# A transformer block with 32 experts on one core: the last down weights are loaded at the start, slots are added in place, down biases are added on the way out of PSUM

## The reference

```python
logits = (hf @ w_router).astype(f32) + b_router.astype(f32)
top_logits, top_idx = lax.top_k(logits, TOP_K)          # 4 of 32
top_w = jax.nn.softmax(top_logits, axis=-1)
...
def expert_block(args):
    xb, e = args
    gu = xb @ w_gate_up[e] + b_gate_up[e]
    gate = jnp.minimum(gu[:, ::2], SWIGLU_LIMIT)
    up = jnp.clip(gu[:, 1::2], -SWIGLU_LIMIT, SWIGLU_LIMIT)
    act = (up + 1.0) * (gate * jax.nn.sigmoid(gate * SWIGLU_ALPHA))
    return act @ w_down[e] + b_down[e]
...
y = jax.ops.segment_sum(ys.astype(f32) * slot_w[:, None], slot_tok, num_segments=n_tok)
```

## Time and profile before

| | us |
|---|---|
| median of 3 runs (1922.38 to 1924.10) | 1923.28 |
| the profiled execution, its time | 1925.91 |
| the profiled execution, its span | 1923.9 |

### The profile page before, as it was taken

The page is one execution under the profiler, slowest core; times in us unless marked ns, Lnnn a source line. Parts: engine busy times, 40 slices in busy tenths (PEclk is TensorE's granted clock), DMA queues, the critical chain, the costliest instruction groups (busy, mean ns, idle before and its releaser), DMA issues.

```text
span 1923.9 us, 40758 instructions
## 1 busy us (share of the span) xinstructions
PE 1877.7 (98%) x17206; PEld 948.9 (49%) x17206; DVE 634.5 (33%) x1168; ACT 333.3 (17%) x596; POOL 262.0 (14%) x305
## 2 busy tenths in 40 slices
PE   7999999999999999999999999999999999999995
PEld 3455555555555444445454545445454545444453
DVE  2463554635623100034231313222231313222226
ACT  3223323323323000021010101101011101101002
POOL 0010010000100000013212122121212122121200
PEclk9999999999999999998999999999999999999998
DMA  9211111111101412337999999999999999999995
GB/s 374 89 66 31 43 45 50 45 51 44 45 10 39 177 66 88 116 131 275 370 420 418 420 417 419 418 420 419 417 420 418 420 418 420 418 419 419 418 400 210
DMA packets 82217, 495.45 MB, mean 258 GB/s; under 512 B 15188, under 2 KB 15868, under 8 KB 28256
## 3 DMA queue, kind: packets, MB, share of 16 engines
q1 hardware_dynamic: 72656, 478.49, 61.6%
q0 software_dynamic: 9488, 15.94, 2.2%
HBM read 478.00 MB, written 24.53 MB: 261 GB/s over the span
## 4 chain that ended last, share of the span: by engine, by line
PE 92%; DVE 3%; DMA 1%; DVEq 1%; SPq 1%; ACT 1%; issue 1%; ACTq 0%
PE ps L1081 34%; PE ps L584 21%; PE ps L1096 17%; PE ps L579 10%; PE ps L604 2%; PE ps L803 2%; DMA arena<-expert_rows 1%; DVE arena L1525 1%; DVE arena L1528 1%; PE ps L1017 1%; PE ps L921 1%; PE ps L916 1%; PE ps L896 0%; PE ps L688 0%; PE ps L773 0%
## 5 line engine op out<-in xcount | busy, mean ns | idle before, releaser
L1081 PE MATMUL ps<-arena 128*32 128x512 f32 x5952 | 646.8, 593 | 2.3 <-DVE arena L1525 2.3
L1081 PEld LDWEIGHTS ps<-arena 128*32 128x32 f32 x5952 | 233.4, 110 | 396.5 <-issue 393.0
L584 PE MATMUL ps<-hT,arena 128*128 128x512 f32 x768 | 350.9, 598 | 1.2 <-DVE arena L1528 0.9
L1096 PE MATMUL ps<-arena,hT 128*32 128x256 f32 x6144 | 339.7, 380 | 8.9 <-DMA arena<-in_w_dn 8.9
L1096 PEld LDWEIGHTS ps<-arena,hT 128*32 128x32 f32 x6144 | 240.2, 110 | 115.2 <-issue 27.6
L1525 DVE TENSOR_TENSOR arena<-ps,arena 128x768 f32<-128x768 f32 x64 | 58.3, 953 | 584.2 <-PE ps L1081 584.2
L584 PEld LDWEIGHTS ps<-hT,arena 128*128 128x128 f32 x768 | 139.0, 191 | 144.3 <-issue 140.1
L2252 POOL DMA_INDIRECT expert_rows<-hT,six x90 | 90.4, 1004 | 684.0 <-ACT hT L1163 665.7
L1163 ACT ACTIVATE hT<-arena 128x768 f32<-128x768 f32 x31 | 48.6, 1567 | 434.0 <-DMA arena<-h_rows,gix 434.0
L584 PE MATMUL ps<-arena 128*128 128x512 f32 x256 | 118.5, 603 | 4.4 <-DVE arena L1525 2.2
L2240 POOL DMA_INDIRECT arena<-h_rows,gix x93 | 95.3, 1025 | 49.0 <-POOL gix L2237 27.2
(11 more groups left out here) (250 smaller groups left out, 1293.8 us busy)
## 6 DMA issues: line engine op xcount, KB each, us to landing
arena<-in_w_gu SPq DMA_DIRECT2D x256, 1024.0 KB, 15.4
arena<-in_w_dn SPq DMA_DIRECT2D x128, 1024.0 KB
arena<-in_w_pair SPq DMA_DIRECT2D x16, 1024.0 KB, 4.9
arena<-in_w_merge SPq DMA_DIRECT2D x16, 1024.0 KB, 4.8
expert_rows<-oaT SPq DMA_DIRECT2D x4, 2048.0 KB, 25.1
arena<-expert_rows SPq DMA_DIRECT2D x16, 512.0 KB, 14.4
arena<-in_x SPq DMA_DIRECT2D x8, 512.0 KB, 6.8
arena<-in_w_qb SPq DMA_DIRECT2D x4, 768.0 KB, 4.5
```

The source lines that it names most:

```text
L584: ins = pe.matmul(region(name)[:, cols], lhsT, rhs, start=(k == 0), stop=(k == n - 1))
L1081: ins = pe.matmul(gu[32 * j:32 * (j + 1), g, :], columns[:, g, k, :], ring[k][:, 512 * j:512 * (j + 1)], start=(k == 0), stop=(k == KD - 1))
L1096: ins = pe.matmul(yd[32 * j:32 * (j + 1), g, 0:256], aT[:, g, 2 * c + k, :], ring[8 + c][:, D * k + 256 * j:D * k + 256 * (j + 1)], start= ...
```

## The change

- **Last down weights.** Expert 31's four down chunks get four buffers of their own (`last_down`, in memory that is free after the router). SP loads them while expert 0 runs: two behind the storing of the last normed rows, two behind the collecting products, all ahead of the loads of the slot table. The last down products (`last_expert_down`) write to the banks of the up products and read their columns from a buffer of their own (`last_aT`).
- **Down bias.** `expert_rows` on VectorE replaces ScalarE's `rows_out`: a small copy and a transpose spread the bias of the expert along rows, and one addition takes the products out of PSUM. `tile_bias`, `weight_columns`, `wmT`, `bb4` and the loads of `bdn` go.
- **Slots.** They are added into `x2` in place of `acc`. VectorE adds slots 0 and 1 ahead of the last activations and slots 2 and 3 between the last two `expert_rows`. Rows of extra blocks go to a table of their own (`late_rows`), which is cleared at the start as well.
- **End.** `AWAY` goes: for each tile `add_parts`, `root`, `finish` one after another on VectorE. The masks signal per expert (`joins_done`).
- **Rows.** The normed rows are written in a permuted order (four strided instructions per tile), so that gathered rows can be transposed directly; ScalarE's `permute` goes. `first_tokens` collects expert 0's rows with tokens as output rows; VectorE transposes them out of PSUM. `table_places(3)` comes behind that transpose, `table_places(2)` ahead of `choose(3)`.
- **Mixer.** `token_rows` and GpSimd's sources go. `along_rows` (a VectorE transpose of a vector spread over 32 columns) makes the same rows; the decays' part (`decay_arguments`) runs at the end of the scan before.

```diff
@@ sync
+            last_down_weights(0)
+            ready(sp, f"lg{NT - 1}")
+            last_down_weights(1)
+            ready(sp, "x0_0", "x0_1")
+            sp.wait_ge(h2_st, 16 * NT)
+            last_down_weights(2)
+            last_down_weights(3)
             sp.wait_ge(table_set, 16 * NT * TOPK)
...
-            for k in range(2):
-                early_slot(k)
-            down_weights(NE - 1, NE - 1)
-            for k in range(2, TOPK):
-                early_slot(k)
+            for k in range(TOPK):
                 sp.wait_ge(gu_used, 8 * (NE - 1) + 2 * k + 2)
                 sp.wait_ge(scattered, 16 * QUADS * min(NE - TOPK + 1 + k, JOINED[0]))
@@ tensor
+            def last_expert_down():
+
+                pe.wait_ge(last_down_in, 64)
+                pe.wait_ge(gu_free, NE)
+                pe.wait_ge(aT_done, NE)
+                for c in range(4):
+                    down_products(last_aT, last_down[c], c, into=gu)
@@ vector, mixer
+            def decay_arguments(i):
+
+
+                along_rows(gc_rows, gc_half[:, i])
+                dv.drain()
+                tt(dt_, gc_rows, fac[:, i, F_GC, :].unsqueeze(2).broadcast_to([P, NC, CHUNK]), ALU.subtract)
+                dv.drain()
+                dv.tensor_scalar(dt_, dt_, 0.0, None, ALU.min).then_inc(arg_done, 1)
@@ vector, router
-                stt(h2[:, t, :], x2[:, t, :], r4[:, 1, t:t + 1], nrow).then_inc(h2_done, 1)
+                for j in range(4):
+                    quarter = slice(256 * j, 256 * (j + 1))
+                    natural = lambda a: a[:, quarter].rearrange("p (m b) -> p m b", b=KD)
+                    ins = stt(h2[:, t, quarter].rearrange("p (b m) -> p m b", b=KD), natural(x2[:, t]), r4[:, 1, t:t + 1], natural(nrow))
+                ins.then_inc(h2_done, 1)
@@ vector, experts
+            def expert_rows(n, e, into=ys, products=yd, passed=0):
+
+
+                dv.tensor_copy(down_now, down_columns[:, bass.ds(8 * e, 8)])
+                dv.drain()
+                dv.transpose(down_rows, down_now.unsqueeze(2).broadcast_to([P, 8, 32]))
+                dv.drain()
+                dv.wait_ge(dn_used, 4 * n + 4)
+                if into is ys and not first(n):
+                    dv.wait_ge(scattered, 16 * QUADS * (n - passed))
+                tt(into.rearrange("p (g s) -> p g s", g=QUADS), products[:, :, 0:256],
+                   down_rows.unsqueeze(1).broadcast_to([P, QUADS, 256]), ALU.add).then_inc(ys_done, 1)
@@ vector, end
+            for k in range(2):
+                early_slot(k)
             activations(NE - 1)
-            activation_columns(NE - 1)
-            dv.wait_ge(row_in, 48)
+            dv.transpose(last_aT.rearrange("p g b m -> p (g b m)"), act.rearrange("p g f -> p (g f)")).then_inc(aT_done, 1)
+            dv.wait_ge(row_in, 32)
...
-            dv.drain().then_inc(wm_done, 1)
-            for k in range(TOPK - 1):
-                dv.wait_ge(slot_in[k], 16 * NT)
-                add_slot(k)
-                dv.sem_inc(early_sums, 1)
+                dv.drain().then_inc(joins_done, 1)
+            expert_rows(NE - 2, NE - 2)
+            for k in range(2, TOPK):
+                early_slot(k)
+            expert_rows(NE - 1, NE - 1, into=last_ys, products=gu)
...
             for t in range(NT):
-                dv.wait_ge(rows_in[t], 48)
-                add_rows(TOPK - 1, t)
-                dv.drain()
-                add_parts(acc, t).then_inc(sum_done, 1)
+                add_parts(t).then_inc(sum_done, 1)
                 dv.sem_inc(bo_kept, 1)
-                if t:
-                    root(t - 1)
-            for t in range(AWAY, NT - 1):
+                root(t)
                 finish(t)
```

More of the change, by code:

```diff
@@ L47 @@
 JOINED = (NE - 2, NE - 1)
-AWAY = 2
 SMALL = 128 + ROWS
@@ L249, in build @@
         osb, WT = U, ar3(28.5, 2, SEQ)
-        sg, sa, dt_, cm, qk = (chunks(29.5 + n / 2) for n in range(5))
+        gc_rows, beta_rows, dt_, cm, qk = (chunks(29.5 + n / 2) for n in range(5))
         vnew = ar3(30.5, 2, P)
@@ L1076, in up @@
                     pe.wait_ge(chunk_in[k], 16 * n + 16)
-                    if first(n) and k % 4 == 0:
-                        after(f"x0_{k // 4}")
+                    if first(n) and k == 0:
+                        after("x0_0")
+                        after("x0_1")
                     for g in range(QUADS):
@@ L1085, in up, with down_products, down @@
                         beside[k]()
-            def down(n):
+            def down_products(columns, weights, c, into=yd):
+                for k in range(2):
+                    for g in range(QUADS):
+                        for j in range(4):
+                            ins = pe.matmul(into[32 * j:32 * (j + 1), g, 0:256], columns[:, g, 2 * c + k, :],
+                                            weights[:, D * k + 256 * j:D * k + 256 * (j + 1)],
+                                            start=(c == 0 and k == 0), stop=(c == 3 and k == 1))
+                ins.then_inc(dn_used, 1)
+            def down(n, loads_before=0):
                 if not first(n):
@@ L1452, in _ @@
             ac.activation(e4[:, :, :], e4[:, :, :], ACT.Exp).then_inc(e4_done, 1)
-            for b in range(2):
-                ready(ac, f"x0_{b}")
-                copy(first_xT[:, :, 4 * b:4 * b + 4, :], region(f"x0_{b}")[:, 0:4 * ROWS].rearrange("p (b g m) -> p g b m", b=4, g=QUADS)).then_inc(frees(f"x0_{b}"), 1)
-            def permute(n):
-                ac.wait_ge(gathered, 16 * QUADS * n)
-                if not isinstance(n, int) or n > 1:
-                    ac.wait_ge(xT_done, n - 1)
-                copy(xgp.rearrange("p (g b m) -> p g m b", g=QUADS, b=KD), xg.rearrange("p (g m b) -> p g m b", g=QUADS, b=KD)).then_inc(permuted, 1)
             def gate(n):
@@ L2115, in _ @@
             spread_bias(1)
-            with dv.Fori(1, NE - 1) as n:
+            activations(1)
+            token_columns(2)
+            activation_columns(1)
+            expert_rows(0, 0)
+            spread_bias(2)
+            with dv.Fori(2, NE - 1) as n:
                 activations(n)
@@ L2163, in _ @@
                         activation_columns(j + NE)
+                        expert_rows(j + NE, e, passed=len(JOINED))
                 dv.wait_ge(again_in, 16 * NT * TOPK)
-                for k in range(TOPK - 1):
+                for k in range(TOPK):
                     add_slot(k)
```

274 lines of the change are left out of this document (116 added, 158 removed).

## The result

Eleven runs of each: the changed kernel takes 1927.06 us (1925.42 to 1928.98), the kernel before 1923.64 (1922.16 to 1925.45). The ratio is 1.0019, with a 95% interval of 1.0012 to 1.0027: about 3.4 us slower. Timed again in two more comparisons the ratio was 1.0018 (1.0009 to 1.0027) and 1.0016 (1.0007 to 1.0025).

A forecast was written before the change was run, and what follows sets the result against it. TensorE, gapless through the experts' loop, was taken as the bound, DMA second. Mixer -3.8, router -3.1 and end +6.7 sum to -0.2 us, giving 1923.1 us on the median; range 1913 to 1931.

The forecast's parts named there:

- its own bound of 0.2%: Whole kernel: a difference within 3.8 us can't be told from no change; 1919.4 to 1927.1 us counts as the same.
- the signs: Wrong if TensorE's gap behind expert 30 is under 10 us, up products wait for chunks, or table loads land after 896.
- The bound and the loop: Experts' loop: TensorE gapless at 30.96 us per expert; VectorE's extra 1.5 us per expert hidden; 3.7 us queue slack holds.
- The queue's estimate: DMA entering the loop: 10.0 us moved loads plus 3.1 less 13.2 idle, about 0; queue as long as before within 2.
- The mixer: Head pairs ahead of the router: fewer products and VectorE operations, less eight added copies; 3.8 us gained, bounds 0 and 7.9.
- the hold that it weighed and set aside: Mixer's tiny VectorE operations: a quadrant change holds the next instruction; by that rule the gain is about 1 us smaller.
- Router to second expert: From first expert's row collection to the second expert's start: first expert 5.8 us earlier, second 3.1; bounds 6.4 and -2.
- rival (c): Router and mixer: table late behind moved loads, or small mixer gains absent; 3 to 5 us lost, 1927.5 us; chance 0.15.
- The end: Behind expert 30's down products: TensorE waits for VectorE's slot additions and activations instead of weights; 6.7 us lost.
- The sum: Whole kernel: -3.8 - 3.1 + 6.7 = -0.2 us, 1923.1 us on the median; forecast's chance 0.45.
- (a): Rival at the end: slots land early, the new wait is short and the weight wait goes; 1914.5 us; chance 0.20.
- (b): Rival in the loop: DMA queue never recovers from the moved 10.0 us; 1929 us with 6 us left; chance 0.20.

The follow-up runs named there:

- e7: Changed kernel with the four last down loads made a second time behind expert 1's up weights, TensorE waiting for all eight: 1938.29 us, ratio 1.0036.
- e6: Kernel before with the mixer's edits alone; router, loop and end as before: 1926.84 us beside 1930.32, ratio 0.9982.
- e9: Changed kernel, unedited, timed again with a profile of another execution: 1927.37 us.
- e10: Changed kernel, unedited, timed again with another profile, beside two edited versions on one chip: 1926.91 us.
- e2: Changed kernel with the loads of the last two quarters of the last down weights issued behind the slot table's loads: 1930.1 us, ratio 1.0006.
- e12: Changed kernel with the last down weights' loads put back at the end: 1924.81 us beside the changed kernel's 1926.91, ratio to before 1.0002.
- e1: Changed kernel with VectorE adding slots 0 and 1 behind expert 30's output rows, not ahead of the last activations: 1917.22 us, ratio 0.9943.

## Why the prediction was wrong where it was

The forecast of 1923.1 was 3 to 4 us low: it said a fraction of a microsecond faster, and the kernel got 3.4 us slower. By its own bound of 0.2% the result, 1927.06, sits at the edge between the same and slower; the interval of that comparison leaves no doubt of the sign. None of the signs came by which it would have called itself wrong: the gap is 17.55 us, no up product waits for a chunk, and VectorE uses the table at 892.26, ahead of 896. The mechanism it named, two gains ahead of the loop paid back by VectorE's new wait, is what the traces show. Two terms were off, and a third was right in part by luck.

**The bound and the loop: right.** Periods of 30.96 us on both sides, no wait in the loop, landings of 25.6 where about 25 was forecast. The first expert starts 13.6 us behind the last tile's transposes instead of 19.0, near the 5.8 less that was estimated. The queue's estimate (10.0 + 3.1 - 13.2, about 0) fits, and e7 confirms the limit of 28.4.

**The mixer: right in size, in part by luck.** Forecast 3.8; 3.5 by e6's time, 5.1 by the traces. The thirteen traces with the new mixer end it anywhere from 862.3 to 866.0 and only one has the old, so the 5.1 could be 2 us off. Inside the term two errors stand against each other. The eight small copies take 1.49 us, not 0.95, and the eight tiny products of a pair take 1.32:

```profile
69.17 1.49 DVE L1568 COPY gc_half<-fac 32x32 f32<-32x32 f32 x8
...
240.37 1.32 DVE L1479 TENSOR_TENSOR beta_half<-fac,r 32x8 f32<-32x8 f32 x8
...
242.52 0.17 DVE L1657 TENSOR_SCALAR lf<-r 128x8 f32<-128x8 f32 x1
```

Each of these copies lasts 0.175 us and starts 0.19 after the one before it, so nothing overlaps. The sixteen copies of the kernel before last 0.174 and start 0.115 apart, but the prediction misread them: by the order of their loops they change quadrant three times in all, where the eight change at every step. So the hold that it weighed and set aside is there. Against that, "two GpSimd products go too" was priced at nothing. In the kernel before VectorE's small operations beside them are long:

```profile
245.10 1.05 POOL L2205 TENSOR_TENSOR arena<-mkc,lf 128x512 f32<-128x512 f32 x1
245.16 1.01 DVE L1673 TENSOR_SCALAR lf<-r 128x8 f32<-128x8 f32 x1
```

The same operation takes 0.17 us in the changed kernel, and another beside GpSimd's first product takes 1.05. In the three pairs behind the first some 2 us of VectorE's time go to this in the kernel before, and they go away with GpSimd's products.

**Router to second expert: the term that failed.** Forecast 3.1; the first pair of traces gives 0.8 (45.3 to 44.5), e9 and e10 2.1 and 1.5. Counted from the last tile's transposes, the gathered rows were to be there 37.4 us on (906.1 less 868.73) and are there at 40.5, so 3.1 later than forecast. Two steps failed.

The larger one is the time of the last table write. The prediction's "the last table writes start behind the row transpose and end about 0.8 earlier" means 18.2 (before: 19.0). It goes out at 20.3, 2.1 later than that: GpSimd has stood 6.66 us for VectorE's addresses of the last tile when it starts the four writes at 879.56. VectorE makes them behind the row transpose, and that waits for the collecting products. In all twelve traces with the new order this write goes out 19.3 to 22.1 us behind the transposes, with the weights early or late, so the moved loads have no part in it.

The smaller one is where the moved loads were put: "two of the moved 1 MB loads go ahead of the table's loads on SP's queue" priced the delay of the table's *loads*, at 2.1 us. What they delay are the table's *writes*, GpSimd's, on another queue, through the DMA engines that they keep busy. The loads wait 2.7 us longer for the write and bring the rows after 15.4 instead of 15.0, so 3.1 stand where 2.1 were allowed. Over the seven traces the interval is 4.6 on average, 2.5 over before's: the price was nearly right, its place was wrong. This is rival (c)'s place, with another victim. The steps behind the rows took 3.9 instead of 4.8. Together 2.1 + 1.0 - 0.9, the 2.2 to 2.3 us that the term is short.

The prediction weighed the Trainium skill (DMA: Bandwidth & Descriptors, section "Queues, rings and completion order") here: on a DMA engine several queues take turns. The queues of the changed kernel in 884 to 885:

```profile
q1 hardware_dynamic: 58, 0.43, 102.6%
q0 software_dynamic: 16, 0.00, 1.1%
```

That is 58 weight packets on 16 engines, 0.28 us each; a table write has 32 packets, two an engine. By turns alone a write would be held some 0.6 us, an estimate; the runs show 2 to 3. So taking turns by itself does not account for what a small write waits beside a full queue; what does was not shown.

**The end: 1.6 us short.** Forecast 6.7 lost, the traces give 8.3 (67.15 us from expert 30's down products to the end of the span, against 58.8). 1.1 of it is one step: slot 0 was to be there 1.3 earlier against TensorE's work, since no 0.5 MB load goes ahead of it; its addition starts 11.3 us after expert 30's down products begin, against 11.5 for the full count before. From slot 0 to the end the prediction's steps give 55.3, the trace 55.9. One trace is a draw here as well: in e9 the end loses 7.0 us and slot 0 comes after 10.0, as forecast, in e10 it loses 10.5 and slot 0 comes after 12.1.

**The sum.** -5.1 - 0.8 + 8.3 = 2.4, where -3.8 - 3.1 + 6.7 = -0.2 stood. The times differ by 1 us more than the traces (3.4), since the profiled execution of before took 1925.91, 2.3 over its median, and that of after 1928.08, 1.0 over. Over the three traces of the changed kernel the mixer gives 5.9, the router 1.4, the loop 0.3, and the end loses 8.6: the router is 1.7 short and the end 1.9, and the mixer gives back 2.1. Where the profiled execution of before spent its 2.3 us over the median is open; a forecast that is summed on one trace and put onto the median carries that much doubt in every term.

**The rivals.** (a) is out: slot 0 comes at 1870.4, not near 1859, and the gap is 17.55 us. (b) did not occur, but e7 and e2 put the loop past its limit and paid, in e7 10.1 us at loop and end for 10.0 of DMA. Missing was a view of the three together. The gain from the table and the slack of the queue are one budget: in e2, where loads behind the table's won time ahead of the loop, the kernel kept none of it. And the change's two halves were not priced one by one. Moving the weights costs 2.1 us (e12), because the order on VectorE hides what it would bring; that order costs 9.7 (e1).

## What to carry to other kernels

When a wait is removed, look at what else stands in the queue of the engine that feeds the next step. Here VectorE waited in order for slot 0, whose data lands late, with work behind it that was ready. That took back more than the early loads could give, and moving two lines behind that work was worth 10 us. When loads are moved into an idle stretch, list the small transfers of *all* queues whose completion somebody waits for in that stretch, not only those behind them on the same queue. For a chain of small writes, count when the addresses of the last one are ready. And a gain ahead of a loop whose DMA is full counts only as far as the queue's slack (here under 3 us of 28.4) goes. Where one stage differs by some microseconds between executions, a term of 1 or 2 us needs more than one trace.

## What the runs showed of the hardware

- The loads that wait for GpSimd's small indirect writes (32 packets each) are issued 2.15 to 2.45 us after the last write on all but idle DMA engines, 4.2 to 5.4 beside the last of four queued 1 MB loads, and 4.0 once with one instruction transfer of 1.2 us on one DMA engine.
- The stretch between router and experts differs between executions. The new one took 40.0 to 44.5 us in the twelve traces that have it. In the shortest (e12) the granted clock stayed at 1.00, the upper level, and the first expert's first 72 records took 7.93 us; in the changed kernel's first trace it was at 0.50, the lower level (1.2 GHz), from 875 to 880, and they took 10.08. The old one took 45.3 and 52.1 us, and 5.7 of these 6.8 us are two waits whose end the profile doesn't name. Whether either is why the kernel before moves more between comparisons was not shown.
- VectorE's norm of the last tile took 2.10 us as four quarters with strided operands, where one plain instruction of the same size takes 1.28. What the split and the stride cost each was not separated.
- In the kernel before, two of VectorE's 128x8 operations took 1.05 and 1.01 us while GpSimd's 128x512 products of 1.04 and 1.05 us ran, at the same place in three head pairs. The second of them takes 0.17 us in the changed kernel, without GpSimd's products.
- Eight copies of 32x32 that change quadrant at every step started 0.19 us apart at 0.175 us each; sixteen of 64x24 that mostly stay in theirs started 0.115 apart at 0.174 each.
